# Weight units of a hybrid decoder block: the matrix products of a unit issued in other orders

## The reference

```python
hn = rmsnorm(h, norm_mix_w)
z, xbc, dt_raw, u, g_a, g_b = split(hn @ w_in)          # 2048 -> 13360 columns
y_a = mamba2_mixer(z, xbc, dt_raw, ...)                 # ends in  y @ w_proj_a   (3072 -> 2048)
y_b = s5_mixer(u, ...)                                  # ends in  y @ w_s5_glu   (1024 -> 4096), val * sigmoid(gate)
h = h + (sigmoid(g_a) * y_a + sigmoid(g_b) * y_b) @ w_out      # 2048 -> 2048
hn = rmsnorm(h, norm_ffn_w)
up = causal_dwconv(hn @ w_up)                           # 2048 -> 11264
h = h + (silu(gate) * val) @ w_down                     # 5632 -> 2048
return rmsnorm(h, norm_final_w)
```

## The kernel before, in words

| phase | units | groups in a turn |
| --- | --- | --- |
| dt, u, zx, bc, gate | 4, 16, 96, 32, 64 | 1, 2, 4, 4, 2 |
| proj | 48 | 2 |
| glu | 32 | 2 |
| out | 32 | 2 |
| up | 176 | 2 |
| down | 88 | 4 |

## Time and profile before

### The profile page before, as it was taken

One profiled execution on the slowest core, in us unless ns is written; L12 is line 12 of the kernel. 1 busy time (PEld: TensorE's weight loads), 2 busy tenths in 40 slices (PEclk: granted clock), 3 DMA queues, 4 the chain that ended last, 5 costly groups with the idle time before them and its releaser, 6 DMA issues.

```text
span 1808.6 us, 30327 instructions
## 1 busy us (share of the span) xinstructions
PE 1776.9 (98%) x9998; PEld 1513.1 (84%) x9998; DVE 1381.5 (76%) x1953; ACT 959.2 (53%) x1216; POOL 146.7 (8%) x216
## 2 busy tenths in 40 slices
PE   7999999999999999999999999999999999999997
PEld 6788888888878888888888888888888888888886
DVE  6799999999988888655787678888888888645444
ACT  6555555555655656565565564444444444433432
POOL 7800000001001010000000100000000000000000
PEclk9999999999999999999999999999999999999998
DMA  6555444455455565555556655555555555555552
GB/s 239 169 176 164 152 163 159 146 172 180 157 177 180 185 197 171 173 188 187 191 190 233 190 183 185 186 186 186 186 184 186 185 186 185 185 188 186 186 186 104
DMA packets 91413, 326.23 MB, mean 180 GB/s; under 512 B 11344, under 2 KB 12368, under 8 KB 91232
## 3 DMA queue, kind: packets, MB, share of 16 engines
q1 hardware_dynamic: 86320, 313.42, 52.5%
q0 software_dynamic: 5040, 12.11, 2.3%
HBM read 323.35 MB, written 2.15 MB: 180 GB/s over the span
## 4 chain that ended last, share of the span: by engine, by line
PE 89%; POOL 3%; DVE 3%; ACT 2%; issue 2%; DMA 1%; SPq 0%; DVEq 0%; ACTq 0%; POOLq 0%
PE psum L1324 56%; PE psum L1325 28%; PE psum L1361 2%; PE psum L1369 1%; DVE dec L1077 1%; POOL s5p L294 1%; PE psum L1408 1%; ACT whi L407 1%; POOL s5p L295 1%; POOL s5p L304 1%; DMA craw<-in_s_c 1%; DVE dec L1083 1%; PE psum L1409 0%; ACT dec L583 0%; POOL iota L311 0%
## 5 line engine op out<-in xcount | busy, mean ns | idle before, releaser
L768 DVE TENSOR_TENSOR wlo<-raw,whi 128x1024 fp32r<-128x1024 f32 x588 | 719.5, 1228 | 363.1 <-ACT whi L407 351.7
L407 ACT ACTIVATE whi<-raw 128x1024 fp32r<-128x1024 f32 x588 | 620.2, 1057 | 561.5 <-PE psum L1325 552.5
L1324 PE MATMUL psum<-act,whi 128*128 128x512 f32 x1792 | 645.3, 403 | 2.3 <-DVE ub L774 2.3
L1324 PE MATMUL psum<-nw,whi 128*128 128x512 f32 x1552 | 548.8, 399 | 4.3 <-DVE wlo L768 4.1
L1325 PE MATMUL psum<-act,wlo 128*128 128x256 f32 x1792 | 501.4, 280 | 0.0
L1325 PE MATMUL psum<-nw,wlo 128*128 128x256 f32 x1552 | 435.5, 281 | 0.0
L1324 PEld LDWEIGHTS psum<-act,whi 128*128 128x128 f32 x1792 | 336.5, 188 | 97.9 <-DVE wlo L768 11.6
L1324 PEld LDWEIGHTS psum<-nw,whi 128*128 128x128 f32 x1552 | 291.6, 188 | 78.3 <-issue 3.2
L1325 PEld LDWEIGHTS psum<-act,wlo 128*128 128x128 f32 x1792 | 338.2, 189 | 0.8
L1325 PEld LDWEIGHTS psum<-nw,wlo 128*128 128x128 f32 x1552 | 293.1, 189 | 0.0
L1324 PE MATMUL psum<-ff,whi 128*128 128x512 f32 x704 | 248.8, 399 | 0.0
(11 more groups left out here) (180 smaller groups left out, 1480.9 us busy)
## 6 DMA issues: line engine op xcount, KB each, us to landing
raw<-in_w_up SPq DMA_DIRECT2D x176, 512.0 KB, 4.2
raw<-in_w_zx SPq DMA_DIRECT2D x96, 512.0 KB, 3.3
raw<-in_w_down SPq DMA_DIRECT2D x88, 512.0 KB, 4.1
raw<-in_w_gate SPq DMA_DIRECT2D x64, 512.0 KB, 3.3
raw<-in_w_proj SPq DMA_DIRECT2D x48, 512.0 KB, 3.2
raw<-in_w_bc SPq DMA_DIRECT2D x32, 512.0 KB, 3.3
raw<-in_w_glu SPq DMA_DIRECT2D x32, 512.0 KB, 3.2
raw<-in_w_out SPq DMA_DIRECT2D x32, 512.0 KB, 4.2
```

The lines of the kernel that those rows point to most:

```text
L407: fn(whi[:, s, :], raw[:, s, :], ACTF.Copy).then_inc(hi_ready, 1)
L768: V.tensor_tensor(wlo[:, s, :], raw[:, s, :], whi[:, s, :], ALU.subtract).then_inc(lo_ready, 1)
L1324: mm(psum[:, b + t, :], whi[:, s, cols], x, start=first, stop=False)
```

## The change

A table `ORDER` gives, for each phase and each group r of a turn, the order of the unit's matmuls. A phase that it lacks keeps "pair", the order of before.

- pair: high, low for each k and t, as before
- highs first: the 8 highs, then the 8 lows
- tile by tile: all of column tile 0 (high, low for k 0 to 3), then all of tile 1
- row: for each k, the two highs, then the two lows
- thirds: as pair, but the high of 512 columns is issued as two matmuls of 256 columns with the same weights, so each pair has three matmuls and three weight loads

```diff
+ORDER = {"proj": ("pair", "highs first"), "glu": ("thirds", "row"), "out": ("row", "tile by tile"),
+         "up": ("highs first", "thirds"), "down": ("pair", "row", "thirds", "tile by tile")}
...
-                for k in range(4):
+                def rows(k):
                     row = 4 * q + k
-                    x = act[:, row + (KT if name == "down" and row >= KT else 0), :]
-                    first, last = q == 0 and k == 0, q == quads - 1 and k == 3
-                    for t in range(1 if name == "dt" else 2):
-                        cols = slice(k * L + t * P, k * L + t * P + P)
-                        mm(psum[:, b + t, :], whi[:, s, cols], x, start=first, stop=False)
-                        ins = mm(psum[:, b + t, L:2 * L], wlo[:, s, cols], x[:, 0:L], start=False, stop=last)
+                    return act[:, row + (KT if name == "down" and row >= KT else 0), :]
+
+                def cols(k, t):
+                    return slice(k * L + t * P, k * L + t * P + P)
+
+                def high(k, t):
+                    return mm(psum[:, b + t, :], whi[:, s, cols(k, t)], rows(k), start=q == 0 and k == 0, stop=False)
+
+                def high_parts(k, t):
+                    first = q == 0 and k == 0
+                    mm(psum[:, b + t, 0:L], whi[:, s, cols(k, t)], rows(k)[:, 0:L], start=first, stop=False)
+                    mm(psum[:, b + t, L:2 * L], whi[:, s, cols(k, t)], rows(k)[:, L:2 * L], start=False, stop=False)
+
+                def low(k, t):
+                    return mm(psum[:, b + t, L:2 * L], wlo[:, s, cols(k, t)], rows(k)[:, 0:L], start=False,
+                              stop=q == quads - 1 and k == 3)
+
+                order = ORDER.get(name, ("pair",) * per)[r]
+                tiles = range(1 if name == "dt" else 2)
+                if order == "highs first":
+                    for k in range(4):
+                        for t in tiles:
+                            high(k, t)
+                    for k in range(4):
+                        for t in tiles:
+                            ins = low(k, t)
+                elif order == "tile by tile":
+                    for t in tiles:
+                        for k in range(4):
+                            high(k, t)
+                            ins = low(k, t)
+                else:
+                    for k in range(4):
+                        if order == "row":
+                            for t in tiles:
+                                high(k, t)
+                        for t in tiles:
+                            if order == "pair":
+                                high(k, t)
+                            if order == "thirds":
+                                high_parts(k, t)
+                            ins = low(k, t)
                 ins.then_inc(unit_used, 1)
```

## The result

The changed kernel takes 1816.12 us (median; 1812.73 to 1818.53), the kernel before in the same sessions 1810.84 us. The ratio is 1.0039, 95% interval 1.0026 to 1.0051: slower, by 5.3 us by the medians and by 7 us by the ratio (5 to 9 us by its interval). One run of the 16 of the kernel before, 2170.16 us, lies far above the others and is not in the ratio, which goes by fast runs. The forecast was 1809.6 us, 1.6 us less than before, and the measured change goes the other way and is larger.

A forecast was written before the change was run, and what follows sets the result against it. The prediction took PE's matmul starts to bound the kernel from proj on. Thirds' -1.6 us, all other terms 0, on the 1808.6 us span, plus the 2.6 us to the median, gave 1809.6 us; range 1795 to 1833.

The forecast's parts named there:

- PE sets the pace from proj on, no wait appears, 1008 matmuls more: From proj on, time is a sum of matmul starts; about 1008 more matmuls and loads, no wait from 755 to 1790 us.
- Thirds, 3 x 117 = 351 ns: Split pairs in glu, up and down: three 256-column matmuls at 117 ns each, -1.6 us in all.
- twice and more for twice the columns: In up and proj, a high is 18 ns over its unstretched time, a low 7 to 8, so surplus goes by columns.
- Rival A: Weight products: surplus belongs to each matmul and its load, so a split pair pays a third portion; +19.3 us, chance 0.18.
- Rival B: Weight products: surplus comes from alternating 512 with 256 columns; runs of one kind cost 0.215 and 0.11 us; -52.3 us, chance 0.08.
- The high behind a wait: Evidence against alternation as the cause: with no matmul before it, a high still takes 38.97 - 38.74 = 0.23 us.
- Rival C: Split units: PE's instruction supply becomes the bound, six instructions a pair; about +80 us, 1891 us, chance 0.06.
- Highs first and row, 0 us: Reordered units from proj on: taken as 0; bounds -24.2 to +7.2 us for highs first, -5.3 to +2.3 for row.
- Patterns, 0 us, bound to a stage: Pairs take 353.5 ns in up and down, 346.5 in proj, glu, out; switching gives -8.6 to +5.4 us, taken as 0.
- The 2.6 us between span and median: Profiled span 1808.6 us lies 2.6 below the runs' median 1811.2; the same difference was added to the forecast.
- The signs: Changed profile: lows 0.115 to 0.12 us apart, highs 0.23 to 0.24, split three 0.35 in sum, stages within 1%.
- the two things that were to refute the prediction: Stage up differing by more than 8 us, or the time leaving 1795 to 1833 us.

## Why the prediction was wrong, and where it was right

The sum was of the right kind, and one of its terms had the wrong size and sign. With 353.5 and 346.5 as the prices of a pair, thirds came out at +7.4 us instead of -1.6, and the other orders at some -2 instead of 0; together +5.4, and +5.3 was measured. That the two figures meet so well is in part luck, since the prices come from single traces and the patterns moved too: in the trace of the changed kernel the plain pairs of proj cost 1.0 us more, and the time ahead of proj is 1.9 us shorter.

- *PE sets the pace from proj on, no wait appears, 1008 matmuls more.* Right in all points, so the sum over starts was the right sum.
- *Thirds, 3 x 117 = 351 ns.* This is the step that failed. A split pair takes 360.0 in every stage, +6.5 on 353.5 and +13.5 on 346.5 in place of -2.5 and +4.5. By the step's own sum that is 6.5 x 880 + 13.5 x 128 = +7.4 us, and the runs show +7.1 and +7.2. The error was the reading "twice and more for twice the columns". It compared a high with a low that alternate, and there, in up, a low takes 0.117 in both patterns and the high the rest, 0.230 or 0.236. In runs of one kind a high has 14 ns over 213 and a low 13 over 107. I had taken 0.117 as the price of 256 columns; it is the price of 256 columns between two of 512.
- *Rival A.* Its mechanism was the right one, a surplus for each matmul with its load, but its price was too high in up: 373 instead of 360, since it shared out all of the 29 ns, of which 7 belong to the alternation and go with the split. From the 346.5 stage it gave 363, three more than measured. The reason it gave, a competition between load and stream, is not shown: narrower loads helped beside 256 columns only, and 32 wide less than 64. The prediction had A at 0.18, and set it aside for the same reading of the highs and lows on which its own term rests.
- *Rival B* had a point: alternation does cost up to 7 ns a pair. But the runs are at 230 and 119, not at 215 and 110, and 1758.9 us is far off. The high behind a wait was a weaker witness than it seemed: its recorded start is 38.63 us (0.50 us long), 0.34 before the low, and the 0.23 counts from the start of the low weights' load at 38.74.
- *Rival C* is refuted up to 60 ns an instruction by the kernel that splits every pair.
- *Highs first and row, 0 us.* Measured 349.1 and 348.4: -4.4 and -5.1 ns against 353.5, +2.6 and +1.9 against 346.5. Within the bounds given. At these prices they come to -3.0 us; the kernel without thirds shows -2 us, with the plain pairs of proj and glu in the upper pattern (352.9 and 353.2 in its trace).
- *Patterns, 0 us, bound to a stage.* That a stage may fall into either was foreseen. That it is by chance from run to run, and that the trace of before was one draw of several, was not. The 2.6 us between span and median that I carried over are smaller than what one such draw moves.
- *The signs.* Lows behind lows at 0.119 and highs behind highs at 0.230 came as said. The three of a split pair take 0.360, halfway between the forecast's 0.35 and A's 0.37. Up is 0.4% longer and down 0.1%, but glu 2.2%, outside the 1% given. Neither of the two things that were to refute the prediction happened: up moved by 1.9 us of the 8 allowed, and the time stayed in 1795 to 1833. Both were too wide to tell the forecast from rival A.
- The rule of the Trainium skill ("TensorE: Matmul & The Clock Gate", section on the back-to-back issue gap), N/2.4 + 2.5 ns, which the section gives for a matmul by itself, makes 109 ns of 256 columns and 216 of 512. The weight matmuls do not keep it: in steady runs of one kind they take 120 and 227, and no order gets a pair under 346.6. Its forecast for the split, +2.5 ns a pair, had the right sign and a third of the size.

## What to carry to other kernels

Where PE is never late, count starts: the price of splitting a moving operand is one more fixed surplus with one more load, here 13 ns a matmul (7 where the pairs ran in the upper pattern, which the split ends), and it is not to be read off a stream in which long and short alternate. Take the price of a shape from a run of that shape, or measure one unit of it.

Look at a periodic stage in more than one trace before a few nanoseconds a pair are put down to the place. Where two patterns exist, an order with one fixed pattern (here two highs, two lows: 1798.5 us against 1810.9 by the medians) can win both time and spread, though not against the best draws of the other (1797.97).

## What the runs showed of the hardware that was not expected

- Settled distances lie on a grid: 113.3, 120.0, 173.3, 226.7 ns for one matmul in a run of its kind and 340.0, 346.7, 353.3, 360.0 for a pair are all multiples of 6.67 ns. The two patterns of a pair are neighbours on it. The single matmuls within a pair or in row order (112.5 to 119.2 and 230 to 236 ns) are not on it, nor are float32 matmuls, at 215 and 109 ns.
- The same program gives 1799.6 or 1810.8 us at the same granted clock of 1.00, and 7.9 of the 11 us lie in the pattern in which its long stages run. In the three traces of it the pattern lasts at least until other matmuls break the stream.
- Weights half as wide save 7 ns beside a 256-column matmul and nothing beside one of 384 or 512, and a quarter as wide saves less than half as wide (118 against 113 ns).
